# Two-layer second block: gate columns projected with the weights stationary, rotation and memory rows moved ahead of the last projection, fewer constant products

## What is computed

```python
def token_mixing(hx, hc, w_in, conv_w, conv_b, b_gates, attn_sink, g_att, g_ml, w_out, rope, with_ctx_out):
    qa_x, ka_x, va_x, qm_x, km_x, vm_x, om_x, gt_x = split_columns(hx @ w_in)
    qa_c, ka_c, va_c, qm_c, km_c, vm_c, om_c, gt_c = split_columns(hc @ w_in)
    q = apply_axial_rope(qa_x.reshape(B, S, ATT_HEADS, ATT_HEAD_DIM), rope)
    k = apply_axial_rope(ka_x.reshape(B, S, ATT_KV_HEADS, ATT_HEAD_DIM), rope)
    att_x = window_attention(q, k, v, k_ctx, v_ctx, sink_g)
    qx_, kx_, vx_, ixf, fxf, ixb, fxb = mlstm_inputs(qm_x, km_x, vm_x, gt_x, conv_w, conv_b, b_gates)
    h_xf, _ = mlstm_chunkwise(qx_, kx_, vx_, ixf, fxf, st_f)
    h_xb, _ = mlstm_chunkwise(flip(qx_), flip(kx_), flip(vx_), flip(ixb), flip(fxb), st_b)
    out_x = merge_groups(att_x, h_xf + flip(h_xb), om_x, g_att, g_ml, w_out)

g = GATE_CAP * jnp.tanh((gt + b_gates) / GATE_CAP)    # 16 gate columns: 4 gates x 4 heads
```

## Time and profile before

| | us |
|---|---|
| median of three runs | 2790.33 |
| lowest, highest | 2790.19, 2812.11 |
| the profiled execution's own time | 2794.95 |
| its span, first to last instruction | 2793.2 |
| mean granted clock of TensorE | 0.956 of full speed |

### The profile page before, as it was taken

The page is one execution under the profiler, slowest core; times in us unless marked ns, Lnnn a source line. Parts: engine busy times, 40 slices in busy tenths (PEclk is TensorE's granted clock), DMA queues, the critical chain, the costliest instruction groups (busy, mean ns, idle before and its releaser), DMA issues.

```text
span 2793.2 us, 38514 instructions
## 1 busy us (share of the span) xinstructions
PE 2591.0 (93%) x14797; PEld 2133.8 (76%) x14842; DVE 1680.9 (60%) x1791; ACT 1286.7 (46%) x1552; POOL 511.4 (18%) x406
## 2 busy tenths in 40 slices
PE   6989999999999988779999989886999999999998
PEld 4657998768997865568889967574887887887886
DVE  4546774456765356643222253656888888887886
ACT  4434344444433254422222133342677667666674
POOL 1002541003522000022003420000312311312311
PEclk9989999999999988899999998896999999999999
DMA  5564554555552200012222221010898898898895
GB/s 200 183 237 160 213 210 146 180 204 171 217 193 87 92 16 9 15 54 98 91 105 91 76 77 76 8 59 28 330 350 332 323 356 334 321 356 327 321 355 193
DMA packets 71419, 502.40 MB, mean 180 GB/s; under 512 B 8176, under 2 KB 8944, under 8 KB 11344
## 3 DMA queue, kind: packets, MB, share of 16 engines
q1 hardware_dynamic: 70128, 495.83, 47.8%
q0 software_dynamic: 1120, 4.14, 0.5%
HBM read 498.89 MB, written 1.05 MB: 179 GB/s over the span
## 4 chain that ended last, share of the span: by engine, by line
PE 85%; DVE 7%; ACT 5%; issue 2%; POOL 1%; DMA 0%; DVEq 0%; ACTq 0%; SPq 0%
PE ps L411 81%; PE ps L451 2%; ACT ring_hi L1437 1%; POOL h_r L1327 1%; DVE h L2029 1%; PE ps L1172 1%; DVE areaA L2021 1%; DVE h L2027 1%; ACT extra_r L1575 0%; ACT h L1515 0%; DVE ring_r L2051 0%; DVE temp L2114 0%; DVE h L2579 0%; DVE ring_r L2782 0%; DVE h L2618 0%
## 5 line engine op out<-in xcount | busy, mean ns | idle before, releaser
L1437 ACT ACTIVATE ring_hi<-ring 128x2048 fp32r<-128x2048 f32 x427 | 806.6, 1889 | 549.6 <-PE ps L411 544.9
L2782 DVE TENSOR_TENSOR ring_r<-ring,ring_hi 128x2048 fp32r<-128x2048 f32 x264 | 626.1, 2382 | 135.0 <-ACT ring_hi L1437 134.2
L411 PE MATMUL ps<-ring_hi,extra_r 128*128 128x512 f32 (+3 forms) x1872 | 632.3, 393 | 32.8 <-POOL h_r L1327 13.7
L2051 DVE TENSOR_TENSOR ring_r<-ring,ring_hi 128x2048 fp32r<-128x2048 f32 (+3 forms) x163 | 386.0, 2368 | 221.7 <-ACT ring_hi L1437 208.3
L411 PE MATMUL ps<-extra_r,ring_hi 128*128 128x256 f32 (+1 forms) x1416 | 458.5, 324 | 31.4 <-POOL h_r L1327 20.5
L411 PE MATMUL ps<-h_r,ring_hi 128*128 128x256 f32 (+1 forms) x1416 | 452.8, 320 | 0.0
L411 PE MATMUL ps<-extra_r,ring_r 128*128 128x256 f32 (+1 forms) x1416 | 452.7, 320 | 0.0
L411 PE MATMUL ps<-ring_r,extra_r 128*128 128x512 f32 (+3 forms) x1168 | 447.6, 383 | 0.0
L411 PEld LDWEIGHTS ps<-ring_hi,extra_r 128*128 128x128 f32 x1872 | 361.6, 193 | 107.0 <-POOL h_r L1327 17.8
L411 PEld LDWEIGHTS ps<-extra_r,ring_hi 128*128 128x128 f32 x1416 | 271.4, 192 | 55.3 <-POOL h_r L1327 23.6
L411 PEld LDWEIGHTS ps<-h_r,ring_hi 128*128 128x128 f32 x1416 | 271.7, 192 | 18.5
(11 more groups left out here) (349 smaller groups left out, 3385.1 us busy)
## 6 DMA issues: line engine op xcount, KB each, us to landing
ring<-in_experts SPq DMA_DIRECT2D x264, 1024.0 KB, 4.9
ring<-in_stream SPq DMA_DIRECT2D x202, 1024.0 KB, 4.9
ring<-in_stream SPq DMA_DIRECT2D x4, 512.0 KB, 3.3
areaB<-in_consts POOLq DMA_DIRECT2D x3, 512.0 KB, 4.8
ring<-in_stream SPq DMA_DIRECT2D x2, 576.0 KB, 3.9
res<-in_xT SPq DMA_DIRECT2D x1, 1024.0 KB, 8.1
res<-in_ctxT POOLq DMA_DIRECT2D x1, 1024.0 KB, 6.9
out_xT<-h SPq DMA_DIRECT2D x4, 256.0 KB, 2.1
```

The source lines that it names most:

```text
L411: return pe.matmul(o, l, r, start=start, stop=stop, skip_group_check=True)
L1437: return act.activation(dst, src, ACT.Copy)
L2051: L.tell(TTN(ring_lo[:, s, 0:n], ring[:, s, 0:n], ring_hi[:, j % HIS, 0:n].bitcast(F32), ALU.subtract), "weights_lo")
L2782: TTN(ring_lo[:, s, :], ring[:, s, :], ring_hi[:, j % HIS, :].bitcast(F32), ALU.subtract).then_inc(sig("weights_lo"), 1)
```

## The change

- The gates are projected after kv, with the weights stationary. The 16 columns are laid out as one chunk of 128 columns, in which gate g's four columns stand eight times over from column 32g on, so that gate g comes out on partitions 32g to 32g+3. 24 matmuls with 512 moving columns take the place of 96 with 16, of the copy and of the 16 transposes. The chunk is 0.5 MB, where it was 64 KB.
- Tanh, Exp and Ln of the gates follow at once on ScalarE, before the SiLU of the convolution; the two Exp come together and then the two Ln.
- `ro`, `kdup` and `brow` move from the memory of `h` to that of `mix2`, and `mrow` to the place of the forget gates.
- VectorE rotates after the convolution and before it copies mv; the transposes to `aqT` and `akT` stand between mv and o; the scans stand after the `aqT` copies, and `lcols` and its Exp between o and the attention. The sigmoid of o stands before that Exp.
- After the attention the memory loop follows directly.
- `wait_h` keeps its ten constant products only once per half of the tokens, in all blocks of the program; the other constant products named above (30, 6, 1, 30 and 2) go. In all, 308 of 490 go.

The streams of SyncE and GpSimd are otherwise the same. The diff, cut to its core:

```diff
-        ro = area(hflat, 0, TT, 512)
-        kdup = area(hflat, 1024, 4, AG, 2, AD)
-        brow = area(hflat, 0, 2, 2 * T)
-        mrow = area(hflat, 1024, 2, 2 * T)
+        ro = area(areaA, 7184, TT, 512)
+        kdup = area(areaA, 8208, 4, AG, 2, AD)
+        brow = area(areaA, 9232, 2, 2 * T)
+        mrow = gates[:, 1::2, :]
...
-                if k == 0:
+                if k == 0 and warmed[0] < h_tiles[0] + hf + 1:
+                    warmed[0] = h_tiles[0] + hf + 1
                     keep_warm(u, 10)
...
                 project(f"kv{l}", w, 512, 768, both, l == 1)
+                rows_ = [Piece(*w, 0, D, 2304 + 4 * g, 2308 + 4 * g) for g in range(4) for _ in range(8)]
+                v = split_chunk(rows_, "p (k c) -> p k c", k=8)
+                u = take("gates", l)
+                for k in range(KD):
+                    m = mm3(ps[:, u.bank, :], lambda s: v[s][:, k, :], lambda s: hs[s][:, :, k, :], k == 0, k == KD - 1)
+                full(m, u)
+                release_with(u)
...
                 project(f"mv{l}", w, 1280, 1792, both)
-                project(f"o{l}", w, 1792, 2304, both if l == 0 else xs)
...
+                pe.wait_ge(sig("att_rope"), 2 * (l + 1))
                 for t in both:
                     if t < 2 or l == 0:
                         u = take("aqT", l, t)
-                        if t == 0:
-                            keep_warm(u, 30)
-                            pe.wait_ge(sig("att_rope"), 2 * (l + 1))
...
-                attend_pairs(l)
-
+                project(f"o{l}", w, 1792, 2304, both if l == 0 else xs)
+
+                pe.wait_ge(sig("lrows"), l + 1)
                 u = take("lcols", l)
-                keep_warm(u, 30)
-                pe.wait_ge(sig("lrows"), l + 1)
...
                 full(m, u)
+                turn[0] = 0
+                attend_pairs(l)
```

More of the change, by code:

```diff
@@ L1838, in _ @@
                     evacuate(L, copy, hi_upto, j + 2 * i, j + 11, tag, a, b, tiles, 0, dst, "proj_act")
+                u = look(act, "gates", l)
+                for g in range(4):
+                    ins = act.activation(gates[0:4, g, :], ps[32 * g:32 * g + 4, u.bank, :], ACT.Tanh,
+                                         bias=cols[0:4, COLS["b_gates"] + 4 * l + g:COLS["b_gates"] + 4 * l + g + 1],
+                                         scale=1.0 / CAP)
+                    if g < 3:
+                        L.step(ins)
+                    else:
+                        free(L, ins, u)
+                hi_upto(j + 7)
+                for d in range(2):
+                    f = gates[0:4, 2 * d + 1, :]
+                    L.step(act.activation(f, f, ACT.Exp, scale=-CAP))
+                for d in range(2):
+                    f = gates[0:4, 2 * d + 1, :]
+                    L.step(act.activation(f, f, ACT.Ln, bias=1.0))
+                act.sem_inc(sig("gates_ready"), 1)
                 for c in range(4):
-                    hi_upto(j + 7 + c // 2)
+                    hi_upto(j + 8 + c // 2)
                     L.wait("conv2", 4 * l + c + 1)
@@ L1843, in _ @@
                     L.tell(act.activation(v, v, ACT.Silu), "conv_done")
[L1844 to L1856 removed]
+                (tag, a, b, tiles, dst), last = after
+                evacuate(L, copy, hi_upto, j + 7, j + 11, tag, a, b, tiles, 0, dst, "proj_act")
+                for g in range(AG):
+                    u = look(act, "akT", l, g)
+                    free(L, copy(akT[:, g, :], ps[:, u.bank, :]), u, "akT")
+                tag, a, b, tiles, dst = last
+                evacuate(L, copy, hi_upto, j + 9, j + 11, tag, a, b, tiles, 0, dst, "proj_act")
                 L.wait("proj_dve", PROJ[f"o{l}"])
@@ L1861, in _ @@
                 act.sem_inc(sig("o_ready"), 1)
-                for g in range(AG):
-                    u = look(act, "akT", l, g)
-                    free(L, copy(akT[:, g, :], ps[:, u.bank, :]), u, "akT")
+                L.wait("lc_ready", l + 1)
+                L.tell(act.activation(temp[:, 736:800], temp[:, 672:736], ACT.Exp, scale=-1.0), "lem_ready")
                 attend_pairs(l)
-                L.wait("lc_ready", l + 1)
-                L.tell(act.activation(temp[:, 64:128], temp[:, 0:64], ACT.Exp, scale=-1.0), "lem_ready")
-                lc = temp[:, 0:64].rearrange("p (t w d h) -> p t w d h", t=4, w=2, d=2)
+                lc = temp[:, 672:736].rearrange("p (t w d h) -> p t w d h", t=4, w=2, d=2)
                 steps, tiles = lsteps(l), range(4) if l == 0 else range(TT)
@@ L2559, in _ @@
                     dve.sem_inc(sig("att_rope"), 1)
+                (tag, a, b, tiles, dst), last = after
+                evacuate(L, copy, lo_upto, j + 7, j + 11, tag, a, b, tiles, 1, dst, "proj_dve")
                 for t in (range(4) if l == 0 else range(TT)):
@@ L2884 @@
     out = nc.dram_tensor("out_xT", (P, KD, T), F32, kind="ExternalOutput").ap()
-    A["stream"] = nc.dram_tensor("in_stream", (sum(I[w].size for w in STREAMED),), F32, kind="ExternalInput").ap()
+    A["stream"] = nc.dram_tensor("in_stream", (sum(I[w].size for w in STREAMED) + 2 * D * (P - 16),), F32, kind="ExternalInput").ap()
     feed["in_stream"] = _np.concatenate([laid_out(I, piece) for piece in build(nc, A, out)])
```

54 lines of the change are left out of this document (11 added, 43 removed).

## The result

| | before | after |
|---|---|---|
| median, us (runs) | 2797.45 (4) | 2731.41 (4) |
| lowest, highest | 2790.19, 2812.11 | 2729.49, 2733.89 |
| the profiled execution | 2794.95 | 2729.90 |
| mean granted clock | 0.956 | 0.953 |

The ratio is 0.9767, 95% interval 0.9737 to 0.9798: faster, by some 66. The forecast was 2709, its range ended at 2731: the gain was overrated by about a quarter, although the part on which most of the working was spent came out larger than forecast.

A forecast was written before the change was run, and what follows sets the result against it. TensorE was taken as the bound (85% of the chain), with serial work in both mixings; 27 + 28 + 19 + 3 + 4 = 81 off the profiled 2794.95 gave 2714, and the median 4.6 lower 2709, range 2694 to 2731.

The forecast's parts named there:

- Up to the attention: Both mixings, to the attention's first exponential: it comes 27 us earlier in layer 0 and 28 in layer 1.
- the sets' 3.0 and 6.5: Mixing projections: dropping sets of ten constant products saves 3.0 us on TensorE's path in layer 0, 6.5 in layer 1.
- The wait of 2.1 ahead of mv's second chunk in layer 0: TensorE waits 2.1 us because VectorE splits that chunk only after the taps and half the rotation.
- The one of 3.7 in layer 1: TensorE waits 3.7 us for the second convolution chunk, whose rounding on ScalarE stands behind the gates' Tanh.
- The 6.6 behind the end of o: Layer 0, end of o to first exponential: VectorE's last copy, then ScalarE's table loads, sigmoid and small Exp, 6.6 us.
- From the attention to the memory loop: Scans and `lcols` leave this stretch; the mask's load then sets the first exponent, 9.5 us earlier, 19 over both layers.
- Constant products in the attention and the memory loop: Removing the single ones in the attention and those ahead of `lo` gains 4 us, within +10 to -11.
- the memory loop gets colder: Rival, chance 0.17: without its constant products the memory loop runs more at half clock, giving 2727.
- Constant products in the first block, and the reference: First block's two layers drop one set each, taken as 3 us; sum taken off the profile's 2794.95, median 4.6 lower.
- splits didn't become a bound: Rival, chance 0.09: VectorE and ScalarE bound the projections, some 4 us a layer, giving 2717.
- the moved work wasn't waited for: Rival, chance 0.06: TensorE waits for the rotation or the rows ahead of o or `lcols`; 15 us gives 2724.
- the clock wasn't lost throughout: Rival, chance 0.03: full clock lost from each attention's start to its memory loop's end, giving about 2820.

The follow-up runs named there:

- lo_back: The changed kernel with the two constant products ahead of each `lo` accumulation of the memory loop put back (48 in all): 2713.3 us.
- shift48: The changed kernel with 48 small constant products of 16 columns added on TensorE ahead of the first projection: 2722.2 us, ratio 0.9711 to before.
- before_lo_cut: The kernel before without the two constant products ahead of each accumulation of the memory loop: 2796.3 us, against 2802.7 unedited (0.9981).
- null_after: The changed kernel, unedited, profiled a second time: 2733.8 us, ratio to before 0.975.

## Why the prediction was right and wrong, by its steps

- **Up to the attention: right, 4 and 3 too small.** Forecast 27 and 28 (the first exponentials), measured 31.2 and 30.7 from the start of the mixing. The gates' 5.5 holds (914.14 to 919.61), the sets' 3.0 and 6.5 were 3.2 and 5.8. The transposes to `aqT` and `akT` took 2.5 (963.66 to 966.20), not 4. The wait of 2.1 ahead of mv's second chunk in layer 0 was 0.19. The one of 3.7 in layer 1 was 1.44 (a table load of 1.28 charged behind G + 0 stood ahead of it), the 0.7 was 0.90. The 6.6 behind the end of o were 5.2, by the sigmoid's table.
- **From the attention to the memory loop: right.** Forecast 9.5 in each layer, measured 9.8 and 10.7; the load is what is late next. "Had the mask been there already it would be 3 more each": it was 2.3 and 2.5 at that place and, with the loops, 11 to 14 in all.
- **Constant products in the attention and the memory loop: the step that failed, wrong in sign.** The term took 4 off the time, from the shares of the earlier trace rows in the chain of the kernel before, within +10 to -11. Measured: 0 for the attention (up to 6 if the idles in the experts are set against it), about +9 for those ahead of `lo` (lo_back against shift48). In the kernel before their removal costs nothing (before_lo_cut). What the step had wrong is that a share read there holds in the loop as the reordering leaves it, where TensorE is granted 0.66 to 0.74 without them. The rival "the memory loop gets colder" named mechanism and place and gave 2727; it should have had more weight, since the earlier trace rows showed half clock there already. The lengths given as its sign, 63 and 36, were not those of whole loops, so it couldn't be read off: from the first exponent on the loops went from 85.1 to 83.1 and from 49.0 to 51.3.
- **Constant products in the first block, and the reference: the other step that failed.** The sets together were sized right (12.5, measured 11 to 14), the 3 for the first block alone can't be told from none. But the sum took everything off one profiled execution, whose first block was 12 shorter than the mean of its own code's five, and off a median of three runs that lies 11 under that of 19.
- **What no step had:** idles of 1.6 to 2.1 in the experts that come and go with the number of instructions ahead of their loop, 2 of the 6.8 in the first profile and 5.7 in null_after.
- **The count.** On the profiled executions 81 was forecast and 65 came: 8.4 better up to the exponents, 12.4 worse in the first block (+9.4 for -3), 4.3 worse in the memory loops (+0.3 for -4), 7.8 worse elsewhere. The remaining 6 of the 22 lie in how each profile stands to its median (-4.6 taken, +1.5 found).
- The other rivals: splits didn't become a bound, the moved work wasn't waited for, and the clock wasn't lost throughout (0.97 and 0.95 over the attentions). Against the median of 19 runs the change gained 70. Beside that the forecast of 81 is 11 too much: 13 for the memory loop (a cost of 9 in place of a gain of 4) and a few in the experts, less the 8.4.

## What to carry to other kernels

What a constant product costs or gains is a property of the order around it: the same two ahead of each `lo` gained nothing before the change, about 9 behind a late mask, and nothing with the mask early. So remove the wait first (here a mask loaded a stage earlier), and then try whether the products can go. When a change takes instructions out ahead of a hardware loop, look at that loop's rows and the packets of kind "instruction" in the new profile, and test with a few small instructions put in elsewhere, before the difference is put down to the edit. A sum over stages should rest on more than one profile of before where the clock dips: the same code's first block differed by 20.

## What the runs showed of the hardware

- With 14358 products in the program TensorE idled 1.6 to 2.1 behind the thirteenth product of a pass of the expert loop, in 9 of 12 passes that began with a jump back; with 14382, 14406, 14418, 14438, 14454 or 14546 in none. In every count, and in the kernel before, it idled 1.4 to 2.1 ahead of the first product of such a pass, with a 16 KB packet of instructions 2.7 to 2.9 ahead of it.
- ScalarE's table load goes ahead of its instruction's semaphore wait (913.45 for a Tanh at 919.81), so beside an idle it cost nothing; without one (991.82, the Exp at 993.11) it cost its 1.28.
- With the mask there before the memory loops instead of 4 behind their start, the two loops together took 133.3 instead of 141.5 to 149.3. The two waits are 4.8 of that; layer 0's loop was granted 0.78 instead of 0.66 to 0.74.
- Dips of the granted clock fall differently in unchanged code from profile to profile (one stretch of 20.5 at 0.50 in the first attention, or two).
